# Delta rule's triangular inverse: five levels on compact 32x32 diagonal blocks

## The reference, cut to what matters

```
qc, kc, vc = chunks of l2norm(q)*dk**-0.5, l2norm(k), v
gcum = cumsum(g) in the chunk; decay_mat[i,j] = exp(gcum[i]-gcum[j]) for i>=j, else 0
a_low = strictly lower part of beta_i * (kc kc^T) * decay_mat
sol   = (I + a_low)^-1 [vc*beta, kc*beta*exp(gcum)]     ;  u, w = sol
attn  = (qc kc^T) * decay_mat ; qe = qc*exp(gcum) ; kd = kc*exp(gcum_end-gcum)
for each chunk, with the state s (128x128):
    v_new = u - w s ;  o = qe s + attn v_new ;  s = s*exp(gcum_end) + kd^T v_new
```

## Time and profile before

| | us |
|---|---|
| median of 3 runs | 3841.05 |
| the runs | 3841.62, 3841.05, 3835.45 |
| span of the profiled execution | 3841.7 |
| PE busy, weight load | 3706.6 (96%), 3089.6 (80%) |
| DVE, ACT, POOL busy | 1869.7, 1204.1, 189.9 |
| mean granted TensorE clock | 0.979 |

### The profile page before, as it was taken

How to read it: one execution, slowest core, us unless ns; L and a number is a source line. 1 busy time by engine, 2 the same in 40 slices (tenths; PEclk the granted TensorE clock), 3 DMA queues, 4 the chain that set the end, 5 groups by cost and what they waited for, 6 DMA issues and landing times. The chain is left out here.

```text
span 3841.7 us, 50616 instructions
## 1 busy us (share of the span) xinstructions
PE 3706.6 (96%) x20661; PEld 3089.6 (80%) x20661; DVE 1869.7 (49%) x2537; ACT 1204.1 (31%) x1762; POOL 189.9 (5%) x210
## 2 busy tenths in 40 slices
PE   8899999999999999999999999999999999999998
PEld 8759999977888787877788788878687788878887
DVE  6565434346534425366554643352526655464334
ACT  3353212245212343232232321234423223333222
POOL 0000000000000100001210100010000122000000
PEclk9999999999999999999999999999999999999999
DMA  3102222212222111220002223222122000322222
GB/s 124 56 2 78 99 89 88 77 54 74 99 99 99 66 66 57 97 77 34 1 18 99 77 96 104 88 80 72 55 88 88 34 1 13 104 77 96 97 92 89
DMA packets 49918, 278.64 MB, mean 73 GB/s; under 512 B 10237, under 2 KB 12797, under 8 KB 20538
## 3 DMA queue, kind: packets, MB, share of 16 engines
q1 hardware_dynamic: 48684, 274.29, 21.1%
q10 hardware_dynamic: 1038, 1.56, 0.1%
HBM read 273.57 MB, written 2.22 MB: 72 GB/s over the span
## 5 line engine op out<-in xcount | busy, mean ns | idle before, releaser
L447 PE MATMUL ps<-xs,ffn_w 128*128 128x512 f32 x2112 | 482.6, 390 | 4.4 <-DVE ffn_w L695 1.8
L447 PEld LDWEIGHTS ps<-xs,ffn_w 128*128 128x128 f32 x2112 | 395.6, 188 | 90.6 <-issue 4.8
L447 PE MATMUL ps<-u,mlp_w 128*128 128x264 f32 (+1 forms) x2880 | 454.7, 320 | 0.0
L447 PEld LDWEIGHTS ps<-u,mlp_w 128*128 128x128 f32 x2880 | 415.9, 189 | 37.7
L447 PE MATMUL ps<-hn,mlp_w 128*128 128x264 f32 (+1 forms) x2304 | 363.6, 320 | 0.0
L447 PEld LDWEIGHTS ps<-hn,mlp_w 128*128 128x128 f32 x2304 | 332.3, 188 | 30.4 <-issue 0.5
L447 PE MATMUL ps<-xs,cv_w 128*128 128x512 f32 x1152 | 268.7, 393 | 0.0
L447 PEld LDWEIGHTS ps<-xs,cv_w 128*128 128x128 f32 x1152 | 215.0, 188 | 59.8 <-issue 13.7
L447 PE MATMUL ps<-ff,ffn_w 128*128 128x512 f32 x1056 | 241.2, 390 | 0.0
L447 PEld LDWEIGHTS ps<-ff,ffn_w 128*128 128x128 f32 x1056 | 198.2, 188 | 42.0 <-issue 1.0
L563 ACT CAST ffn_w<-raw 128x2048 fp32r<-128x2048 f32 (+1 forms) x74 | 124.3, 1680 | 303.9 <-PE ps L447 264.0
(11 more groups left out here) (456 smaller groups left out, 5240.8 us busy)
## 6 DMA issues: line engine op xcount, KB each, us to landing
raw<-in_w_ffn_up SPq DMA_DIRECT2D x44, 1024.0 KB, 5.0
raw<-in_w_up SPq DMA_DIRECT2D x32, 1024.0 KB, 5.0
raw<-in_w_down SPq DMA_DIRECT2D x32, 1024.0 KB, 5.0
raw<-in_w_conv SPq DMA_DIRECT2D x24, 1024.0 KB, 5.0
raw<-in_w_ffn_down SPq DMA_DIRECT2D x32, 704.0 KB, 4.1
raw<-in_w_mqk SPq DMA_DIRECT2D x10, 1024.0 KB, 5.1
raw<-in_w_qk_even SPq DMA_DIRECT2D x9, 1024.0 KB, 5.0
raw<-in_w_mv SPq DMA_DIRECT2D x8, 1024.0 KB, 4.9
```

The costliest lines, as they stand in the source:

```text
L447: ins = nc.tensor.matmul(bank(u)[:, h, :], w[:, s, wp, k * g.bw + j * P:k * g.bw + (j + 1) * P], g.xs[:, xp, k, h * n:(h + 1) * n], start= ...
```

## The change: what it does

- Levels 1 to 4 work on compact buffers [128, 4, 32]: in each 32-partition strip lie the four chunks' 32x32 diagonal blocks of that strip. `ut` holds u and t side by side, and one VectorE instruction of 256 elements per partition updates both. A product is a 32x32x32 matmul per chunk and strip (`in_blocks`, 16 per head). t is no longer a transpose of u: it gets a product of its own, u^T y.
- Level 0 is made once by VectorE, with its own 32x32 transpose. GpSimd makes the masks' products of all five levels in one instruction (`by_level`).
- Level 5 joins 32-blocks to 64-blocks in two or three 32x32x32 matmuls per chunk (8 matmuls for y and 12 for w and t, per head); its results go with a minus sign straight into u and `ty`.
- Level 6 is the same quarter, then w_turned and scan as before.
- GpSimd copies the diagonal blocks into the full u (`diagonal`), ScalarE cuts the diagonal blocks out of N (`cut`), fills corners and sides.
- The preparation is spread anew (`aside`): the transposes of keys and values of pair i are made in its own levels 1 and 2, in bank 1; the spreads of pair i+1 in levels 2 and 3; its key products in level 5; its query products (`scores`) in the scan. The decay's column bias moves from ScalarE's four instructions to a GpSimd addition (`mg`), so that one exponential does.
- Output copies and squares of pair i-1 come behind the first copy of pair i's level 1.

```diff
+                def in_blocks(e, b, part, lhs, rhs):
+                    for c in range(NCH):
+                        for q in quads:
+                            ins = nc.tensor.matmul(blocks(e, b, part)[q, c, :], lhs[q, c, :], rhs[q, c, :], start=True, stop=True)
+                    return ins
...
+                def update(i, b, e, f, s):
+                    n, ut = f["big_n"][i % 2], f["ut"][i % 2]
+                    if b < small:
...
+                        pe.wait_ge(s["ut_done"], small * i + b)
+                        in_blocks(e, 0, 0, f["nb"][i % 2][:, b, :, :], ut[:, 1, :, :]).then_inc(s["y_filled"], 1)
+                    elif b == small:
+                        pe.wait_ge(s["ut_done"], small * (i + 1))
+                        for c in range(NCH):
+                            for q, to in ((quads[0], quads[1]), (quads[2], quads[3])):
+                                ins = nc.tensor.matmul(blocks(e, 0)[to, c, :], n[q, c, to], ut[q, 1, c, :], start=True, stop=True)
+                        ins.then_inc(s["y_filled"], 1)
...
+                def apply(i, b, e, f, s):
+                    ut, yc = f["ut"][i % 2], f["yc"]
+                    pe.wait_ge(s["y_copied"], (levels - 1) * i + b)
...
+                    if b < small:
+                        in_blocks(e, 2, 0, yc, ut[:, 0, :, :])
+                        in_blocks(e, 2, 1, ut[:, 0, :, :], yc).then_inc(s["w_filled"], 1)
...
+                def aside(i, b, e, f, s):
+                    after = i < pairs - 1
+                    if b == 1:
+                        pe.wait_ge(s["qe_done"], i + 1)
+                        turn(e, 1, tile_of(1, i, e), s["turned_k"])
+                    if b == 2:
...
+                        turn(e, 1, tile_of(2, i, e), s["turned_v"])
+                    if b == 2 and after:
...
+                        spread(e, s, i + 1, 0, 3)
+                    if b == 3 and after:
+                        pe.wait_ge(s["vb_done"], i + 1)
+                        spread(e, s, i + 1, 1, 1)
+                        pe.wait_ge(s["khat_done"], i + 2)
+                        spread(e, s, i + 1, 2, 3)
+                    if b == 5 and after:
+                        pe.wait_ge(s["kb_done"], i + 2)
+                        each(e, 1, tile_of(1, i + 1, e), f["kb"], s["kk_done"])
...
-                    for b in range(levels):
+                    for b in range(1, levels):
                         for e, f, s in both:
+                            update(i, b, e, f, s)
+                        aside(i, b, *both[0])
+                        for e, f, s in both:
+                            apply(i, b, e, f, s)
+                        aside(i, b, *both[1])
+                        if i and b == 1:
                             for e, f, s in both:
                                 pick_squares(i - 1, e, f, s)
...
+                def updated(i, b, e, f, s):
+                    dve.wait_ge(s["w_filled"], (levels - 1) * i + b)
+                    if b < small:
+                        both_parts = f["ut"][i % 2][:, :, :, :].rearrange("p a c n -> p (a c n)")
+                        nc.vector.tensor_tensor(both_parts, both_parts, ps[:, 4 * e + 2, 0:2 * NCH * HB], ALU.subtract).then_inc(s["ut_done"], 1)
+                    elif b == small:
+                        nc.vector.tensor_scalar(f["ty"][quads[1], :, 0:HB], blocks(e, 2, 1)[quads[1], :, :], -1.0, None, ALU.mult).then_inc(s["t_done"], 1)
+                    else:
+                        nc.vector.tensor_scalar(f["u"][0:HC, :, HC:CHUNK], bank(e, 2)[0:HC, :, HC:CHUNK], -1.0, None, ALU.mult).then_inc(s["u_done"], 1)
...
+                        if c < 2 and i < pairs - 1:
+                            scores(i + 1, 0, *both[c])
```

More of the change, by code:

```diff
@@ L2515, in _, with mask_and_decay @@
             def _(pool):
-                for i in range(pairs):
[L2517 to L2528, removed]
+                def mask_and_decay(i, e, f, s):
+                    if i:
+                        pool.wait_ge(s["arg_done"], i)
+                    nc.gpsimd.tensor_tensor(f["mg"][:, :, :], mask4, wide(NEG_G, 2 * i + e), ALU.add).then_inc(s["mg_done"], 1)
@@ L2530, in _ @@
+                for e, f, s in both:
+                    by_level(0, e, f, s)
+                for i in range(pairs):
+                    for e, f, s in both if i < pairs - 1 else ():
+                        mask_and_decay(i + 1, e, f, s)
+                    for e, f, s in both:
+                        diagonal(i, e, f, s)
+                    for e, f, s in both if i < pairs - 1 else ():
+                        by_level(i + 1, e, f, s)
             @block.tensor
@@ L2542, in quarter @@
                     for c in range(NCH):
[L2543 removed]
+                        ins = nc.tensor.matmul(bank(e, b)[to, c, rows], lhs(rows, c), rhs(rows, c), start=True, stop=True)
                     ins.then_inc(sem, 1)
@@ L2634, in _ @@
[L2634 to L2655, removed]
@@ L2700, in _, with outputs @@
+                def outputs(i):
+                    for e, f, s in both:
+                        act.wait_ge(s["o_filled"], NCH * (i + 1))
+                        nc.scalar.copy(out[:, 2 * i + e, :], ps[:, 4 * e + 3, :]).then_inc(s["o_copied"], 1)
+                        if i:
+                            act.wait_ge(s["picked"], i)
+                        nc.scalar.activation(f["sq"][:, :], ps[:, 4 * e + 3, :], ACT.Square).then_inc(s["squared"], 1)
                 for e, f, s in both:
-                    decays(0, e, f, s, 1)
+                    decays(0, 1, e, f, s)
@@ L2702, in _ @@
+                for e, f, s in both:
+                    cut(0, e, f, s)
                 for i in range(pairs):
+                    after = i < pairs - 1
                     for b in range(1, levels):
                         for e, f, s in both:
-                            act.wait_ge(s["y_filled"], levels * i + b + 1)
-                            if b == levels - 1:
-                                ins = nc.scalar.copy(f["y"][HC:CHUNK, :, 0:HC], bank(e, 0)[HC:CHUNK, :, 0:HC])
-                            else:
-                                ins = nc.scalar.copy(f["y"][:, :, :], bank(e, 0))
@@ L2710, in _ @@
-                            ins.then_inc(s["y_copied"], 1)
-                        if i == 0 and b in (3, 4):
-                            decays(1, *both[b - 3])
-                        if 0 < i < pairs - 1 and b in (2, 3):
-                            decays(i + 1, *both[b - 2])
+                            copy_y(i, b, e, f, s)
+                        if i and b == 1:
+                            outputs(i - 1)
+                        for e, f, s in both if b == 4 and after else ():
+                            decays(i + 1, 3, e, f, s)
@@ L2715, in _ @@
+                        for e, f, s in both if b == small else ():
+                            corner(i, e, f, s)
+                        for e, f, s in both if b == small else ():
+                            sides(i, e, f, s)
                     for e, f, s in both:
@@ L2721, in _ @@
                             nc.scalar.copy(f["vn"][:, c % 2, :], bank(e, 1)[:, c, :]).then_inc(s["vn_copied"], 1)
-                    for e, f, s in both:
-                        act.wait_ge(s["o_filled"], NCH * (i + 1))
-                        nc.scalar.copy(out[:, 2 * i + e, :], ps[:, 4 * e + 3, :]).then_inc(s["o_copied"], 1)
-                        if i:
-                            act.wait_ge(s["picked"], i)
-                        nc.scalar.activation(f["sq"][:, :], ps[:, 4 * e + 3, :], ACT.Square).then_inc(s["squared"], 1)
+                        if c < 2 and after:
+                            cut(i + 1, *both[c])
@@ L2828, in _ @@
[L2828 to L2835 removed]
+                            updated(i, b, e, f, s)
@@ L2836, in _ @@
+                        for e, f, s in both if b == 3 and after else ():
+                            arguments(i + 1, 3, e, f, s)
+                        for e, f, s in both if b == 5 and after else ():
+                            lower(i + 1, 1, e, f, s)
                     for c in range(NCH - 1):
@@ L2844, in _ @@
                             ins.then_inc(s["s_done"], 1)
+                        if c < 2 and after:
+                            attention(i + 1, 0, *both[c])
+                        for e, f, s in both if c == 2 and after else ():
+                            first_level(i + 1, e, f, s)
                 for e, f, s in both:
```

321 lines of the change are left out of this document (149 added, 172 removed).

## The result

The changed kernel took 3771.3 us (median of 4 runs, 3765.6 to 3780.4) against 3838.3 for the kernel before beside it: a ratio of 0.9823 (0.9806 to 0.9841), 67 us less. 3798 was forecast, 43.5 less; 3771 lies inside the forecast's own range of 3770 to 3830, but only just. The profiled execution has a span of 3763.8 us, 77.9 less than before: it was the shortest run of the changed kernel, and the one of before was the longest.

A forecast was written before the change was run, and what follows sets the result against it. TensorE's queue, nearly always occupied, was taken as the bound. Costed as its work, four pairs take 184.8 us a stage against 207.3 and 205.8: 43.5 us less, 3798 us. Own range 3770 to 3830, overall 3745 to 3890.

The forecast's parts named there:

- The strips overlap: In in_blocks, 32x32 products on the four diagonal tiles were taken to run at once, 8 instructions each.
- X: Price of one in_blocks (16 products, 32 matmul instructions): 0.45 us at 1.2 GHz, 0.25 at 2.4; gain spent at 0.65.
- The row that carried it: Trace of line 1118 before the change: 32 instructions on 64x32 tiles took 2.06 us together, eight running at a time.
- the two-at-a-time rival: In in_blocks, shared bank or queue order lets only two tiles run at once: X = 0.85, 3883 us; chance 0.16.
- The clock: TensorE in the delta stages: 1.2 GHz from level 2 to w_turned, 2.4 GHz in level 1 and the scan.
- the rival of strips: In in_blocks, strips don't overlap: two at a time 3883 us, chance 0.16; one at a time 4063 us, chance 0.10.
- the gaps between shapes: TensorE's pause at each change of tile shape in the levels: 0.2 us at high clock, 0.3 at low; 1.4 a level with asides.
- the rival with the high clock: Delta stages stay at 2.4 GHz all through, levels 2 and 3 at 4.5 us: 49 us less a layer, 3700; chance 0.12.
- What lies beside it: VectorE, GpSimd and ScalarE work beside TensorE in the pairs: hidden, nothing taken; if VectorE's cover goes, 15 us.
- the joints: Rival: in the levels, shape changes, waits through ACT and DVE and asides cost 1 us more each: 3842 us; chance 0.10.

The follow-up runs named there:

- e6: The changed kernel with the loops of in_blocks turned, row strip outer and chunk inner, same 16 products: 3855.0 us, 1.0042 of the kernel before.
- e1: The changed kernel run once more without an edit, as yardstick: 3769.1 us, 0.9825 of the kernel before.
- e5: The changed kernel plus twelve unused in_blocks for each head behind the last pair's scan of each stage: 3805.0 us, 0.9908 of the kernel before.
- e3: The changed kernel plus one unused 128x128 by 512 float32 matmul between y and w products in levels 2 to 4: 3782.8 us, 0.9842 of the kernel before.
- e7: The changed kernel with a pair's output copies and squares issued ahead of the next pair's level 1 again: 3792.8 us, 0.9887 of the kernel before.
- e11: e4 plus the next pair's third spread and decay arguments moved from level 3 to level 4: 3730.4 us, 0.9713 of the kernel before.
- e4: The changed kernel without the t product of levels 1 to 4; VectorE transposes u instead: 3732.8 us, 0.9724 of the kernel before.
- e2: The changed kernel with every y product of levels 1 to 4 issued twice: 3831.8 us, 0.9980 of the kernel before.
- e9: The changed kernel plus 16 one-column products for each head in levels 1 to 4, as many instructions as e2 added: 3835.0 us, 0.9991 of the kernel before.

## Why the prediction was right, and where it was off

**The strips overlap: right, and the size nearly.** X was taken at 0.45 us at 1.2 GHz and 0.25 at 2.4; it is 0.42 and 0.28. The row that carried it (64x32 tiles in different halves) held for four row strips that write one PSUM bank, so the rule of the Trainium skill that row tiles can't share a bank at once (TensorEngine Tiling (Array Packing), Restrictions and Gotchas) did not show as time here. e6, where X is 0.66 to 1.0 us, shows about what the two-at-a-time rival (X = 0.85) would have done: some 17 us slower than before, where its working had 42.

**The clock: the step that failed.** I took 1.2 GHz "from level 2 to w_turned", 33 us of each of three pairs and 24 of the last, 123 a stage. Stretches of the changed kernel, columns as in Rows 6:

```profile
1829.00:1839.00 10.00, 9.46 (x409) 6.34 (x408) 5.98 (x13) 3.03 (x8) 0.00 (x0) 1.00 0.02 5
1843.00:1863.00 20.00, 18.89 (x414) 16.94 (x405) 6.95 (x14) 6.57 (x19) 2.30 (x8) 0.50 0.01 2
1887.30:1893.90 6.60, 5.58 (x233) 4.56 (x232) 3.40 (x7) 2.21 (x6) 0.34 (x2) 0.50 0.02 5
1894.10:1913.05 18.95, 18.34 (x279) 17.33 (x280) 9.41 (x21) 9.47 (x34) 4.87 (x9) 1.00 0.01 2
```

Pair 1 kept 2.4 GHz through levels 1 and 2 and into level 3. Pair 2 (the last two rows) fell in its level 3 as well, but was back at 2.4 GHz when level 5 had just begun, where pair 1 stayed low to the end of `w_turned`. The low time is (1 - clock) / 0.5 of a stretch: with the clock unrounded, 75 and 81 us in the two stages, and the granted clock 0.78 and 0.76 where I expected near 0.6. What a microsecond of it costs can be read from pair 1 in two executions of the same kernel (after, then e1), where only the clock differs much:

```profile
1829.97:1874.05 44.08, 41.18 (x1031) 35.22 (x1030) 21.85 (x42) 15.01 (x47) 7.91 (x12) 0.77 0.02 3
```
```profile
1833.51:1872.60 39.09, 36.86 (x1031) 30.70 (x1030) 21.86 (x42) 15.04 (x47) 7.92 (x12) 0.87 0.01 4
```

20.3 us low against 10.2: 5.0 us longer, 0.5 us a microsecond (0.7 us of it is idle time). 45 us less of low clock than forecast are thus some 22 us a stage (an estimate from this one pair).

**Instruction supply: the term that was missing.** Stalls of 15.7 and 13.1 us a stage stand in no step. The prediction had the fact beside it ("PE issues 192 instructions a level instead of 40"), and used it only for the rival of strips. The trace of before could not show it: its packets lie 13 to 20 us apart.

**What is left: some 10 us a stage, not placed.** 167.4 measured less 184.8 forecast is -17.4; +14.4 of stalls and -22 of clock leave -10 a stage. It is not in the gaps between shapes at the high clock. Level 2 above takes 5.14 us, 4.6 without its stall, and the rival with the high clock had 4.5 for it, gaps and all; a spread still takes 0.65 us to the next start, the figure that the gap was read from the earlier trace rows. By the same working for each pair (an estimate), pairs 0, 1 and 2 leave -1.8, -1.4 and -0.1, and pair 3 -6: its levels 2 and 3 took 3.1 and 2.4 us without their stalls, where 5.8 and 3.4 were priced, at 1.2 GHz. Part of that can be waits at joints, which the sum held and which passed while TensorE stood for instructions anyway; no run separates it. Two errors of one sign (the clock and this rest) and one of the other (stalls) made a sum that missed by 24 us of 67. That 3771 still lay inside the range owes something to luck: the stalls, which the sum did not hold, took back part of what the clock gave.

**Level by level, pair 1**, forecast and measured: level 1 6.0, 4.95; level 2 7.5, 5.14; level 3 7.5, 7.96 (2.1 of it stalls); level 4 3.4, 2.7; level 5 7.1, 6.7; level 6 4.0, 3.5; `w_turned` 3.5, 3.5; scan 10.1, 9.7 (to the next pair's first level at 1873.07); together 49.1, 44.1. From level 4 on, with the low clock there up to the scan, the working holds within 0.7 us a line, and nowhere too short.

**What lies beside it: right.** TensorE never waits long for VectorE's subtraction inside the levels (1 us a stage), GpSimd's diagonal copies are 2.6 us for eight and done before level 6, and ScalarE's cuts are hidden (no wait of TensorE in the stage ends with them). **The rivals**: the joints took next to nothing; the high clock came for part of the time, which is where most of the miss is.

## What to carry to other kernels

Cutting a product into small tiles paid here only with neighbours in the queue in different row strips (e6), and only up to the rate at which instructions arrive: count the matmuls and weight loads of a stretch. Where a long run of them would issue at under some 15 ns each (3.75 us for 256, e5), that count sets the time and not their size; a short run goes from what has arrived, as the first 224 matmuls of e5 did. A stop in the middle of a product with "issue" as its releaser, and instruction packets at even distance, are the sign. Then take instructions away: a transpose by VectorE, which had time for it, in the place of a second product gave 36 us. To place few long instructions between the dense stretches is not shown to help: pair 3, which has fewest of them, stalled most (8.4 us), but to move or add some (e3, e7, e11) did not lower the sum. An estimate that fixes the clock for a whole stretch should carry both levels in its range: the same code took 39 or 44 us. And where a run's time moves, look at its clock before giving the time to the edit, as e7 shows.

## What was not expected of the hardware

- TensorE's instructions came at 256 in 3.75 us in a bare run of them, with no other DMA traffic, while small products issue at 4.4 ns an instruction where nothing holds them (2.4 GHz).
- One-column 32x1 products cost as much as 32x32 ones in the levels: +66 and +63 us for 4096 instructions more, both with 119 to 126 us a stage at 1.2 GHz.
- The order of the same 16 products in four strips changed their time from 0.28 to 0.66 us at 2.4 GHz.
- What keeps the clock down for 20 us in one pair and for 7 in its twin stays open: with the stalls taken away (e4) the low time was 75 us a stage, against 75 to 85 with them, and with more instructions (e2, e9) it was 119 to 126.
